# Moving the weights' buffers by 192 bytes in a kernel of three blocks on one core

## The reference, cut to what matters

```python
def reference(x, c, ctx, ...):
    # layer 0: gated in-projection, mLSTM scans in both directions, pooling, out-projection
    # layer 1: in-projection, layer norm, spatial gating, out-projection
    # both: x * (1 + scale) + shift before, g * y and layer norm behind,
    #       with scale, shift and g = silu(c) @ ada_w + ada_b
    x = first_block(x, c, ctx, ...)
    # latent attention and a gated linear recurrence side by side, w_out,
    # a lookup of experts (top 16 of 128 x 128, 8 heads), a last gate
    return second_block(x, ...)
```

```python
u = peer_u[ec]
act = jax.nn.gelu(jnp.einsum('tkd,td->tk', u, xc))
return jnp.einsum('tk,tkd->td', gc * act, peer_v[ec])
```

## Time and profile before

| | us |
|---|---|
| median of 3 runs | 3753.03 |
| lowest and highest | 3751.19, 3781.72 |
| the profiled execution's own time | 3763.23 |
| its span, first to last instruction | 3761.4 |
| TensorE matmuls busy | 3610.3 |
| VectorE, ScalarE, GpSimd busy | 2091.6, 1562.3, 2039.0 |
| mean granted clock of TensorE | 0.98 |

### The profile page before, as it was taken

The page is one execution under the profiler, slowest core; times in us unless marked ns, Lnnn a source line. Parts: engine busy times, 40 slices in busy tenths (PEclk is TensorE's granted clock), DMA queues, the critical chain, the costliest instruction groups (busy, mean ns, idle before and its releaser), DMA issues.

```text
span 3761.4 us, 71588 instructions
## 1 busy us (share of the span) xinstructions
PE 3610.3 (96%) x30016; PEld 3481.5 (93%) x30016; DVE 2091.6 (56%) x3062; ACT 1562.3 (42%) x1970; POOL 2039.0 (54%) x816
## 2 busy tenths in 40 slices
PE   6999998999999889999999999999999999999998
PEld 3799897979999879999999999999999999999998
DVE  6686456783724465554114679784444666544454
ACT  5413433334344334454444434434444444444453
POOL 0147591008084648789899960007888100188876
PEclk9999999999999999999999999999999999999999
DMA  8557751765653424545455545545555455455543
GB/s 330 191 210 261 277 221 73 299 234 189 251 200 132 147 100 157 180 157 185 175 200 192 192 182 185 179 169 184 196 190 192 179 179 183 180 196 190 192 166 124
DMA packets 98407, 716.37 MB, mean 190 GB/s; under 512 B 11040, under 2 KB 11168, under 8 KB 12064
## 3 DMA queue, kind: packets, MB, share of 16 engines
q1 hardware_dynamic: 97056, 703.65, 51.0%
q10 hardware_dynamic: 1152, 9.87, 0.7%
HBM read 711.38 MB, written 2.10 MB: 190 GB/s over the span
## 4 chain that ended last, share of the span: by engine, by line
PE 83%; DVE 8%; POOL 4%; DMA 2%; ACT 2%; issue 2%; DVEq 0%; SPq 0%; POOLq 0%; ACTq 0%
PE bank L541 54%; PE bank L1055 19%; POOL unit_lo L478 3%; DMA ring<-in_w 2%; PE bank L593 2%; PE bank L696 2%; DVE unit_lo L1775 1%; PE bank L570 1%; PE bank L1006 1%; ACT unit_hi L1102 1%; PE bank L635 1%; PE bank L513 1%; DVE ada_acc L1576 1%; PE bank L805 1%; DVE unit_lo L1659 1%
## 5 line engine op out<-in xcount | busy, mean ns | idle before, releaser
L478 POOL TENSOR_TENSOR unit_lo<-ring,unit_hi 128x1024 fp32r<-128x1024 f32 x806 | 2023.2, 2525 | 1656.7 <-ACT unit_hi L1102 1655.2
L1102 ACT ACTIVATE unit_hi<-ring 128x1024 fp32r<-128x1024 f32 x1204 | 1239.7, 1056 | 1194.7 <-PE bank L541 479.5
L541 PE MATMUL bank<-xl_hi,unit_hi 128*128 128x256 f32 x4688 | 1321.6, 282 | 23.2 <-POOL unit_lo L478 9.9
L541 PE MATMUL bank<-xl_lo,unit_hi 128*128 128x256 f32 x4688 | 1307.5, 279 | 0.0
L541 PE MATMUL bank<-xl_hi,unit_lo 128*128 128x256 f32 x4688 | 1307.0, 279 | 0.0
L541 PEld LDWEIGHTS bank<-xl_hi,unit_hi 128*128 128x128 f32 x4688 | 890.5, 190 | 30.5 <-issue 11.5
L541 PEld LDWEIGHTS bank<-xl_hi,unit_lo 128*128 128x128 f32 x4688 | 888.0, 189 | 0.0
L541 PEld LDWEIGHTS bank<-xl_lo,unit_hi 128*128 128x128 f32 x4688 | 886.8, 189 | 0.6
L1055 PE MATMUL bank<-w_r,unit_hi 128*128 128x256 f32 x4096 | 699.7, 277 | 4.0 <-DVE w_r L2584 4.0
L1055 PEld LDWEIGHTS bank<-w_r,unit_hi 128*128 128x128 f32 x4096 | 619.1, 188 | 4.3 <-issue 4.3
L1055 PE MATMUL bank<-w_r,unit_lo 128*128 128x256 f32 x2048 | 566.8, 277 | 0.0
(11 more groups left out here) (441 smaller groups left out, 5135.0 us busy)
## 6 DMA issues: line engine op xcount, KB each, us to landing
ring<-in_w SPq DMA_DIRECT2D x669, 1024.0 KB, 4.8
resid<-in_xT ACTq DMA_DIRECT2D x1, 2048.0 KB, 15.7
tmp_ctx<-in_ctxT ACTq DMA_DIRECT2D x1, 2048.0 KB, 11.3
sgu_rows<-in_sgr ACTq DMA_DIRECT2D x1, 2048.0 KB, 9.5
rnn_gates<-in_rgw ACTq DMA_DIRECT2D x1, 2048.0 KB, 8.8
out<-resid SPq DMA_DIRECT2D x4, 512.0 KB, 2.6
con<-in_con ACTq DMA_DIRECT2D x1, 512.0 KB, 3.3
con<-in_con ACTq DMA_DIRECT2D x1, 448.0 KB, 7.9
```

The lines of the kernel that those rows point to most:

```text
L478: pool.tensor_tensor(lb[b][:], ring[slot][:, f * HALF:(f + 1) * HALF], hb[b][:].bitcast(F32), ALU.subtract).then_inc(lo_done, 1)
L541: mm = pe.matmul(bank[(s.t0 + tile[m]) % TILES][:, 0:T], w[b][:, (i % 8) * P:(i % 8 + 1) * P], mv[x][:, k, :], start=(k == 0 and w is hb a ...
L1102: act.activation(hb[b][:], ring[slot][:, f * HALF:(f + 1) * HALF], ACT.Copy).then_inc(hi_done, 1)
```

## The change: two small tensors go to the front

`cond` and `tick` are placed first. Every fixed tensor from `ring` to `mod` moves up by 192 bytes, `mrow`, `erow`, `acol` and `rstd` by 64 (`cond` is no longer ahead of them), `lam_s` and the zone of the activations not at all.

```diff
+        cond = fixed("cond", [P, KC, 2], F32)
+        tick = fixed("tick", [1, 1], F32)
         ring = [fixed(f"ring{i}", [P, UNIT], F32) for i in range(RING)]
         hb = [fixed(f"unit_hi{i}", [P, HALF], F32R) for i in range(NBUF)]
         lb = [fixed(f"unit_lo{i}", [P, HALF], F32R) for i in range(NBUF)]
...
         mod = fixed("mod", [P, 96, 2], F32)
-        cond = fixed("cond", [P, KC, 2], F32)
         mrow = fixed("mrow", [64, T], F32)
         erow = fixed("erow", [64, T], F32)
         acol = fixed("acol", [P, 2, 4, 4], F32)
         rstd = fixed("rstd", [P, T], F32)
-        tick = fixed("tick", [1, 1], F32)
         lam_s = fixed("lam_s", [P, KC], F32)
         z0 = (at[0] + 63) // 64 * 64
```

## The result

The changed kernel takes 3886.7 us (median of 4 runs, 3883.3 to 3887.7) against 3763.3 us for the kernel before beside it (3751.2 to 3781.7): a ratio of 1.032, 95% interval 1.027 to 1.037. It is slower by 123 us, above the range that I gave, which ended at 3815. The profiled executions differ by 3887.7 - 3763.2 = 124.5 us.

A forecast was written before the change was run, and what follows sets the result against it. The prediction took TensorE's weight-load and matmul pairs to bound the kernel (matmuls busy 96% of the span). Its five terms, all 0, left the median of 3753 us; own range 3725 to 3785, about one in ten beyond either of 3700 and 3815.

The forecast's parts named there:

- steps 1 to 4: Instructions, addresses, VectorE/ScalarE/GpSimd and DMA: none added or moved, the engines and transfers blind to the new addresses, 0 us.
- step 5: TensorE's weight loads and activation reads at the new addresses: taken as 0 us, between ends of -76 and +79 us.
- the two paces: TensorE's load-and-256-column pairs on L541 and L1055: about 113.3 or 117.8 ns at one clock, kept for a whole run.
- The upper end: TensorE on L541 and L1055: all 19,800 quick pairs go to the slow pace of 117.8 ns, +79 us.
- The slower rival: TensorE pairs: aligned remainders make the two reads meet and the slow pace the rule, full size 3832 us; chance 0.19.
- the 0.9 for the share on the path: L541 and L1055: 2,746 us of chain against 3,040 us of busy time, so 0.9 of it is on the path.
- The lower end: TensorE pairs on L541 and L1055: the weight loads alone set the pace, 111 ns, -76 us.
- slow-paced stretches turn quick: TensorE: only the 5,650 slow pairs turn quick, 23 us less, 3730 us; counted within the no-change chance of 0.60.
- the slower case: Whole kernel slower by more than 1% (37.5 us), through TensorE pairs turning slow; chance 0.19.

The follow-up runs named there:

- E6: Kernel before with cond and tick placed behind unit_lo, so only resid, vec, con and mod move by 192 bytes: 3772.1 us, ratio 1.002.
- E5: Kernel before with cond and tick placed between ring and unit_hi, so ring stays and unit_hi, unit_lo and all behind move by 192 bytes: 3896.9 us, ratio 1.035.
- E4: Separate kernel of only 48-pair bursts (weight load, then columns) at 64 offset combinations, no other engine at work: 120.0 ns at distance 0, 113.3 or 117.8 at 64.
- E2: Kernel before with only cond put ahead of the ring, moving the weights' buffers by 128 bytes while activations stay: 3822.3 us, ratio 1.011.
- E9: Kernel before with all tensors, weights' buffers and activations alike, 16 bytes further: 3742.0 us, ratio 0.991.
- E8: Kernel before with everything, weights' buffers and activations alike, 32 bytes further: 3767.1 us, ratio 1.001.

## Why the prediction was wrong, point by point

**Instructions, VectorE, ScalarE, GpSimd, DMA (steps 1 to 4): right.** Counts are the same and so are the durations of the splits, the copies and the transfers; E6 bears out the residual, the constants and the small tensors. That the ring is needed for the loss is refuted by E5, where it stays, and by E4, in which there is none.

**TensorE (step 5): the mechanism was named, and its value set to 0. This is the step that failed.** I took 0 "because the rows that compare addresses show no difference at all, and those that show a difference have no difference of address in them". Each of the two halves is a true reading from which nothing follows. The rows that compare addresses were of other forms: a load under 256 columns against one under 512, where a pair has some 227 ns and the load's own pace is 112, and plain float32, at half the pace. E4 has plain float32 at all four pairings, as flat as in the earlier trace rows. With 512 columns it shows a difference, 226.7 to 233.3 ns, which the loads' mean duration of the earlier trace rows didn't show; that duration was not a measure of the pair's pace. The form that matters was in the trace at one distance only. What the runs showed in place of the 0: 120.0 ns for nearly every pair at a distance of 0, +124.5 us between the profiled executions. And that the two paces appear at one distance says that the interference has a state, not that the distance has no part in it.

**The upper end: too low by 45 us (+79 against +124.5).** The slower rival named the mechanism that came and had its size wrong: it supposed that the slow pace of the trace is the worst. All quick pairs at 117.8 is what E2 shows, at +50 us between medians and +77 in its profiled execution. The changed kernel has a pace that the trace of before did not contain: 19,800 x (120.0 - 113.3) + 5,650 x (120.0 - 117.8) = 145 us, of which 0.9 is 131; measured are 124.5. The place of the loss held, and the 0.9 for the share on the path roughly: the changed kernel's profiled execution had a mean granted clock of 0.984 against 0.980, an estimate of 13 us in its favour (2.0% of 3761 against 1.6% of 3886), and without that the loss would be near 137 us, 0.95 of the 145. That 137 x 0.9 meets 124 so closely is in part luck.

**The lower end:** the loads' own pace, 111 ns, comes near what 128 columns have (111.7 in E4) but is reached nowhere with 256 columns. The rival "slow-paced stretches turn quick" did not happen here. E9 shows that it can be had by other addresses: -23 us by my sum, -33 measured between medians and -20 between profiled executions.

**The range and the chances.** I gave the slower case 0.19, and I ended the range in the middle of it. With one resource at 96%, in a form whose reads were known to interfere, and a relative shift that the trace had never tried, a value of 0 had nothing behind it but rows of other forms.

**The rule that TensorE's weight loads have a read port of their own** (the page "SBUF — State Buffer" of the Trainium skill, section "A bandwidth-pool intuition that's wrong (but worth ruling out)") would have made the placement worth 0. How many ports there are no run shows, but what I took from the rule doesn't hold: with TensorE alone at work, the same pair takes from 113.3 to 123.4 ns by nothing but their offsets.

## What to carry to other kernels

Where TensorE streams fp32r products of 256 columns with a new 128 x 128 load for each, the byte offset of the stationary buffers against the moving ones is a parameter worth 6% of a pair's time (113.3 to 120.0 ns): try a distance of 64 modulo 256 and start both at an odd multiple of 16. Do it in a kernel of bursts first; one run of 1.6 ms read 224 bursts, and the whole kernel then behaved as the bursts did (E9), while two bursts were too few to go by (E8). And if a row shows two paces for one instruction at one clock, look for the state behind it before calling any edit neutral that touches its operands, and don't take the slower of the two as the worst there is.

## What the hardware showed that I had not expected

- Adding 192 bytes ahead of the weights costs 123 us of 3763, adding 256 nothing that can be told from 0. Shifts of 64 and 128 cost 88 and 50 (all between medians).
- A pair keeps one of a few exact paces over thousands of repetitions: 113.3, 117.8, 120.0 ns. At a distance of 64 there are two for the same addresses, and what ran before chooses.
- At the lower clock (1.2 GHz, granted 0.5) the effect is gone: in all whole kernels nearly all intervals there are 213 or 214 ns, before as after.
- The 512-column form has an order of its own. In L593, where the weights move and the activation is stationary, the changed kernel is a little quicker (60.14 us for 264 instead of 60.70). Start of the stationary operand minus start of the moving one is 192 there before and 0 after; alone, these have 228.9 and 226.7 ns. E2 makes it 64, the slowest alone with 233.3, and its L593 takes 61.86 us.
- What makes the reads meet, and why 16 bytes steady the pace, was not tried beyond the offsets themselves and stays open.
